# A mixture-of-experts kernel: one branch per expert against one per block of matmuls, and a last down tile of full width

## The reference

```python
def swiglu(h, wg, wu, wd):
    return (jax.nn.silu(h @ wg) * (h @ wu)) @ wd

def moe_ffn(h, w_router, w_e_gate, w_e_up, w_e_down):
    logits = jnp.einsum('btd,de->bte', h.astype(jnp.float32), w_router.astype(jnp.float32))
    top_v, top_i = lax.top_k(logits, TOP_K)
    top_w = jax.nn.softmax(top_v, axis=-1)
    gate = ...
    for e in range(N_EXPERTS):
        out = out + gate[..., e:e + 1] * swiglu(h, w_e_gate[e], w_e_up[e], w_e_down[e])
```

## Time and profile before

| what | value |
|---|---|
| median of 3 runs | 4669.5 us (4656.28 to 5200.78) |
| the profiled execution | 4663.14 us |
| its slowest core (3), first to last instruction | 4661.6 us |
| its other cores | 4575.8 to 4638.5 us |
| TensorE busy | 4180.5 us, 90% of the span |
| matmuls of the experts' gate and up (L1364 with wgu) | 7168 |
| matmuls of the experts' down (L1654) | 2072 |

### The profile page before, as it was taken

How to read it: one execution, slowest core, us unless ns; L and a number is a source line. 1 busy time by engine, 2 the same in 40 slices (tenths; PEclk the granted TensorE clock), 3 DMA queues, 4 the chain that set the end, 5 groups by cost and what they waited for, 6 DMA issues and landing times.

```text
span 4661.6 us, 73833 instructions; the slowest of 8 cores (4575.8 to 4661.6 us)
## 1 busy us (share of the span) xinstructions
PE 4180.5 (90%) x25337; PEld 2225.0 (48%) x25337; DVE 1926.7 (41%) x3537; ACT 1964.7 (42%) x2884; POOL 907.3 (19%) x959
## 2 busy tenths in 40 slices
PE   5888988899999999898988899959989999998895
PEld 3444433334444444444433344537638647465571
DVE  3767676752331223758585832442102112111133
ACT  5777687852331213777687742321101111011112
POOL 0111222233200000111222233331111211201101
PEclk9999999999999999999999999979999999999998
DMA  4000211032484331000301132538868977677876
GB/s 115 10 11 1 47 33 38 29 63 41 100 188 83 89 78 46 2 10 2 65 29 38 30 62 38 121 61 152 154 121 143 165 126 141 124 133 132 166 160 207
DMA packets 115186, 390.90 MB, mean 84 GB/s; under 512 B 19040, under 2 KB 30688, under 8 KB 95584
## 3 DMA queue, kind: packets, MB, share of 16 engines
q0 software_dynamic: 63856, 275.09, 33.9%
q1 hardware_dynamic: 50928, 110.52, 7.4%
HBM read 576.85 MB, written 49.61 MB: 134 GB/s over the span
## 4 chain that ended last, share of the span: by engine, by line
PE 74%; DVE 7%; issue 7%; DMA 5%; ACT 5%; POOL 1%; DVEq 0%; ACTq 0%; SPq 0%; POOLq 0%
PE ps L1364 22%; PE ps L712 20%; PE ps L1654 10%; PE ps L826 4%; PE ps L834 4%; PE ps L1423 3%; PE ps L835 3%; ACT PTb L831 2%; PE ps L827 2%; ACT PT L831 2%; DMA wgu<-wE 1%; PE ps L1117 1%; DMA ygt<-yt 1%; PE ps L1142 1%; DMA xr<-x 1%
## 5 line engine op out<-in xcount | busy, mean ns | idle before, releaser
L1364 PE MATMUL ps<-xgT,wgu 128*128 128x256 bf16 (+1 forms) x7168 | 854.4, 283 | 102.7 <-issue 78.0
L1364 PEld LDWEIGHTS ps<-xgT,wgu 128*128 128x128 bf16 x7168 | 710.7, 99 | 246.9 <-issue 109.1
L1374 ACT ACTIVATE sgf<-ps 128x304 f32<-128x304 f32 (+1 forms) x536 | 216.6, 451 | 1019.4 <-PE ps L1364 998.1
L1375 DVE TENSOR_TENSOR aT<-ps,sgf 128x304 bf16<-128x304 f32 (+1 forms) x536 | 248.5, 505 | 931.6 <-PE ps L1364 914.0
L831 ACT ACTIVATE PTb<-ps 128x1024 bf16<-128x1024 f32 x512 | 501.7, 1027 | 91.9 <-PE ps L827 78.4
L831 ACT ACTIVATE PT<-ps 128x1024 bf16<-128x1024 f32 x512 | 502.6, 1033 | 73.5 <-PE ps L827 55.3
L1654 PE MATMUL ps<-wdn,aT 128*128 128x512 bf16 (+1 forms) x2072 | 510.9, 383 | 11.9 <-DVE yst L1671 8.9
L712 PE MATMUL ps<-hT,wm 128*128 128x512 bf16 x1536 | 362.5, 380 | 0.0
L1654 PEld LDWEIGHTS ps<-wdn,aT 128*128 128x128 bf16 (+1 forms) x2072 | 179.6, 98 | 337.0 <-issue 194.1
L1364 PE MATMUL ps<-hT,wf 128*128 128x512 bf16 x1408 | 307.0, 381 | 6.7 <-DMA wf<-wF 5.4
L1302 ACT ACTIVATE sg<-ps,vec 128x512 bf16<-128x512 f32 x192 | 131.9, 689 | 345.3 <-PE ps L712 343.7
(11 more groups left out here) (239 smaller groups left out, 6241.6 us busy)
## 6 DMA issues: line engine op xcount, KB each, us to landing
wgu<-wE POOLq DMA_DIRECT2D x112, 1024.0 KB, 9.7
wdn<-wEd POOLq DMA_DIRECT2D x112, 512.0 KB, 6.9
xr<-x SPq DMA_DIRECT2D x51, 512.0 KB, 5.1
wf<-wF POOLq DMA_DIRECT2D x22, 1024.0 KB, 10.1
ropeA<-ropeA SPq DMA_DIRECT2D x40, 512.0 KB, 4.0
wm<-wM POOLq DMA_DIRECT2D x48, 384.0 KB, 4.5
x<-xr SPq DMA_DIRECT2D x32, 512.0 KB, 3.9
wCh<-wC POOLq DMA_DIRECT2D x8, 1024.0 KB, 8.4
```

The costliest lines, as they stand in the source:

```text
L1364: ins = e.matmul(pk[v * n + i][0][:, 0:b - a], w(v, c, k), rhs(k, a, b), start=(k == 0), stop=(k == 7))
L1374: S.op("act", lambda e, pg=pg, sg=sg, m=b - a: e.activation(out=sg[:, 0:m], in_=pg[0][:, 0:m], func=AF.Silu), reads=[pg[1]], writes=[("sgf ...
L1375: S.op("dve", lambda e, pu=pu, sg=sg, m=b - a, a=a, b=b: e.tensor_tensor(out=out(a, b), in0=pu[0][:, 0:m], in1=sg[:, 0:m], op=ALU.mult), r ...
```

## The change

`choose` loads an expert's level once, before its first group, and keeps it in a register (`levels`). `stretches` no longer makes one stretch per expert: it takes at most 4 operations with levels that follow each other directly on PE, and ends a group where an operation without levels (a transpose) or another expert comes. Each group gets the two nested branches and its three bodies. There are 8 stretches before and 151 groups after: for each expert 14 groups of 64 matmuls for gate and up, and 5 for down (4 for the last expert). The last down tile is no longer as wide as its tokens (48 or 96) but always 128 columns. It runs over into the columns of the next chunk of `aT`, and for the last chunk into 128 columns of padding that POOL zeroes once. The rows of the result beyond the tokens aren't read.

```diff
@@ choose
-        level_ap, level_op = first["sel"][1:]
-        self.waits_for(eng, {level_op}, wm)
-        v = eng.value_load(level_ap)
+        ex, level_ap, level_op = first["sel"]
+        if ex not in self.levels:
+            self.waits_for(eng, {level_op}, wm)
+            self.levels[ex] = eng.value_load(level_ap)
+        v = self.levels[ex]
@@ stretches
-            else:
-                yield order[n:last[sel[0]] + 1]
-                n = last[sel[0]] + 1
+        group = []
+        for idx in self.eng_ops[ename]:
+            sel = self.ops[idx]["sel"]
+            if group and (sel is None or len(group) == 4 or sel[0] != self.ops[group[0]]["sel"][0]):
+                yield group
+                group = []
...
@@ expert_block
-                        w = min(128, n - i * 128)
                         at = i * 128 if i * 128 < h else HALF + i * 128 - h
-                        ins = e.matmul(C.ps[bk[i]][0:w, :], C.aT[:, 4 * q + c, at:at + w], wv[:, c, :], start=(q == 0 and c == 0), stop=(q == NC // 4 - 1 and c == 3))
+                        at += (4 * q + c) * CAP
+                        ins = e.matmul(C.ps[bk[i]][:], C.aTf[:, at:at + 128], wv[:, c, :], start=(q == 0 and c == 0), stop=(q == NC // 4 - 1 and c == 3))
...
@@ moe
-    C.aT = one("aT", [128, DFFE // 128, CAP], BF16)
+    width = DFFE // 128 * CAP
+    C.aTf = one("aT", [128, width + 128], BF16)
+    C.aT = C.aTf[:, 0:width].rearrange("p (c t) -> p c t", c=DFFE // 128)
+    S.op("pool", lambda e: e.memset(C.aTf[:, width:width + 128], 0.0), writes=[("aT", DFFE // 128, 0)])
```

More of the change, by code:

```diff
@@ L141, in __init__ @@
         self.uid = 0
+        self.levels = {}
     def alloc(self, stack, name, shape, dt):
@@ L412, in stretches @@
     def stretches(self, ename):
[L414 to L422, removed]
+        group = []
[4 more added lines that the diff above has]
+                group = []
             if sel is None:
-                yield [order[n]]
-                n += 1
-            else:
-                yield order[n:last[sel[0]] + 1]
-                n = last[sel[0]] + 1
+                yield [idx]
+            else:
+                group.append(idx)
+        if group:
+            yield group
     def run(self, ename, eng, final_waits=()):
@@ L1651, in fn @@
                     for i in range((n + 127) // 128):
-                        w = min(128, n - i * 128)
                         at = i * 128 if i * 128 < h else HALF + i * 128 - h
-                        ins = e.matmul(C.ps[bk[i]][0:w, :], C.aT[:, 4 * q + c, at:at + w], wv[:, c, :], start=(q == 0 and c == 0), stop=(q == NC // 4 - 1 and c == 3))
+                        at += (4 * q + c) * CAP
+                        ins = e.matmul(C.ps[bk[i]][:], C.aTf[:, at:at + 128], wv[:, c, :], start=(q == 0 and c == 0), stop=(q == NC // 4 - 1 and c == 3))
                 return ins
             alts = [lambda e, fn=fn, m=m_, h=h if m_ < CAP else m_: fn(e, n=m, h=h) for m_, h in LEVELS] if sel else None
-            down = S.op("pe", fn, reads=[("wdn", s)] + [("aT", 4 * q + c, i) for c in range(4) for i in range(len(segs))], writes=[("ps", b) for b in bk], alts=alts, sel=sel)
+            down = S.op("pe", fn, reads=[("wdn", s), ("aT", 4 * q + 4, 0), ("aT", 4 * q + 4, 1)] + [("aT", 4 * q + c, i) for c in range(4) for i in range(len(segs))], writes=[("ps", b) for b in bk], alts=alts, sel=sel)
             hook("p2", half * 7 + q)
```

## The result

The change made the kernel slower: the ratio of after to before is 1.030, with a 95% interval of 1.024 to 1.037. The profiled execution took 4803.42 us, against 4663.14 us before. In some executions one half of the chip (cores 0 to 3 or 4 to 7) ran at a lower granted clock than the other; they are left out of every ratio here, which is why ratios and not medians are given, and where a profile is one of them, cores of the other half are read. All cores became slower, and in the profiled execution core 3 is still the slowest.

A forecast was written before the change was run, and what follows sets the result against it. TensorE, busy 90% of the slowest core's span, was taken as the bound. 4663 - 78 (jumps) - 60 (narrow tile) + 190 (code fetch) = 4715 us, plus 6 to the median: 4720 us; range from 4525 less 25 to 4900.

The forecast's parts named there:

- The narrow tile: Last down tile: a 48-wide matmul costs 0.43 us, at 128 columns 0.2165; 60 us saved on core 3.
- The jumps between experts: PE's 8 waits for issue at L1364, one per expert, are removed: 78.0 us saved.
- How the code comes in: TensorE's sequencer holds its 256-instruction block and the next; gate and up groups need 1.58 blocks; some 400 packets on queue 8.
- The size of the added waits: Waits for code in gate and up groups add 190 us; down adds 0, at most 15.
- L: Time from TensorE's sequencer entering a block of instructions to having the next, taken as 5.5 us.
- two bounds: Added gate and up time: 123 us if groups' spare time carries over fully, 227 us without any carrying over.
- rows 8: Profile rows where PE on cores 4 and 6 stops 18 matmuls behind a jump; read as 5.7 and 6.2 us per block.
- The clock: TensorE's lower clock behind gaps, 1.2 GHz, left the same before and after: no time added.
- case D: Rival, chance 0.22: the forecast's mechanism in gate and up with 6.3 us per block; 4831 us, 3.5% slower.
- C: Rival, chance 0.18: a jump into a block still arriving restarts its fetch; 196 us more, 4915 us, 5% slower.
- B: Rival, chance 0.20: instructions are far enough ahead or jumps inside them cheap, nothing added; 4525 us, 3% faster.

The follow-up runs named there:

- the lengths of 2, 4 and 8: The changed kernel with at most 2, 4 (as it stands) or 8 operations in a group: core 3 at 4721.0, 4801.6 and 5026.6 us.
- 1.05 blocks: The changed kernel with two bodies per group, levels 1 and 2 sharing that of level 2: ratio to before 0.984, core 3 at 4597.1 us.

## Why the prediction was wrong

The forecast was 4720 us, within 2%; the profiled execution took 4803.42 us, and the ratio says 3% slower. The range held it, but the forecast had a rise of 1.1% where there is one nearly three times as large.

- **The narrow tile, 60 us.** Right: 58.8 us alone. 140 down matmuls at level 1 take 30.38 us.
- **The jumps between experts, 78 us.** Right that these long gaps go. Wrong that all of it is gained: at the starts of five experts PE then waits 2 to 4 us for `yst`, and at that of the last 18.1 us in place of 11.1. 22 us of the gain (33.1 - 11.1) went there. The prediction didn't say what is late next.
- **How the code comes in.** Right in the main: queue 8 took 369 packets, "some 400"; the waits are in gate and up (176.9 us) and few are in down (21.0 us, where it had "at most 15"); 76 and 9 of them, "a hundred or so of 1 to 5 us". That the sequencer holds one block and the next is what the lengths of 2, 4 and 8 bear out.
- **The size of the added waits, 190 us.** 176.9 + 21.0 = 198 us. Right in size, with some luck: 190 was picked between 123 and 227, and a little too much for gate and up makes up for the nothing of down. It doesn't single out L = 5.5 us. By the prediction's own two bounds, 176.9 us in gate and up go with an L from 5.1 to 5.8 us. Its reading of core 4 in rows 8 is 5.6 us (3857.93 - 3846.4 - 5.91), not 5.7, which changes nothing.
- **The clock, left "on both sides".** This is the step that failed. The reason given, "since new gaps will do the same", would need the new gaps to do as much as the old 8, and there are 85. Gate and up work grew by 56.3 us (910.7 - 854.4), down by 8.5 over the kernel with the tile alone (460.6 - 452.1): 65 us that the sum had at 0. Of these 45.6 and 7.7, 53 us, are work at the lower clock; the other 12 are the last matmuls of more separate runs, which the prediction didn't have either.

With both terms, and `wgu` no longer waited for (-8.8), core 3's span should change by 120 (issue) + 22 + 65 - 9 - 59 = 139 us; it changed by 140. Both are of one execution of each kernel; in a second one of the changed kernel core 3 took 4781.8 us. The time came out near that of case D (4831 us), but not for D's reason: D needs waits of at least 269 us in gate and up, and they were 176.9. C would add 196 us of waits and is out, and so is B, which has none.

## What to carry to other kernels

In this kernel a branch in TensorE's stream cost little where its target lay in the block that runs or the next; what cost was the code that is passed over, since it has to be fetched as well. Count blocks of 256 instructions per stretch of work against 5 to 6 us each beside heavy weight traffic (an estimate from L above): 1.58 blocks for 7 to 8 us of work left 198 us of waits, 1.05 blocks 10 us. Small skipped bodies help, but groups of 2 still took 4721.0 us where the kernel before took 4661.6. When short gaps replace a few long ones, price the clock behind them by their length, and ask which wait the long gap had been hiding.

## What the runs showed of the hardware that was not expected

- A matmul of 512 columns behind a weight load of 48 columns took 0.43 us, behind one of 128 columns 0.2165 us, and the full tile alone saved 0.21 us for each. In the rows the mean durations (397 and 380 ns) hardly show it; the time of the whole run of matmuls does.
- A far jump took 3.5 us at the end of the kernel before and 3.9 us at most with an eighth of the weight bytes, but 4.7 to 8.7 us at `L403` beside the full weights, for the same packet of 16 KB. On core 4 an eighth of the weight bytes took 168 us of waits away.
- A gap of 4.94 us was followed by 3.3 us at a granted clock of 0.53, and on core 3 none of 43 gaps below 2 us was followed by the lower clock.
